# Differential and mLSTM head outputs made with tokens on the partitions, normed per token and then turned; a projection unit in spare banks, products amid halves

## The chip, the cores and the metric

The kernel runs on one core of one Trainium2 chip. The metric is the device time of one execution in microseconds (us), the median of several runs. The profile is of one further execution.

## What is computed

Two transformer blocks, one after the other, on 256 tokens of width 2048 in float32. Most of the work is the projections: x of (256, 2048) times w_in, w_br, w_out, w_up, w_down and the gates of each block. The change touches the outputs of two kinds of heads. In the first block, four differential heads:

```python
attn = (pr[:, :, 0] - lam * pr[:, :, 1])            # two softmaxes
ob = einsum('bhqk,bhkd->bhqd', attn, v)             # (256 tokens, 256 features) a head
ob = rmsnorm(ob, sub_g) * (1.0 - lambda_init)       # over the 256 features of the head
yb = ob.reshape(B, S, 1024) @ w_br_diff
```

In the second block, four mLSTM heads, which the kernel computes in one piece over all 256 tokens (here as weights W that hold all gates and decays):

```python
s = (q @ k.T) * W
h = (s @ v) / max(abs(s.sum(-1)), exp(-m))          # one divisor for each token
ha = rms_norm(h, mlstm_out_g) * sigmoid(mo)         # over the 256 features of the head
x = x + concat([ha, hb], -1) @ w_out
```

## The kernel before

**Blocks and stages.** Every weight block passes through the same pipe. SP's queue loads 128x2048 words into `raw`. A *half* is half of such a load, 128x1024. ScalarE copies the half to `split` as a rounded high part (`hi`, L562), VectorE subtracts to get the low part (`lo`, L1157), and TensorE multiplies high and low parts with X (`blocks`, L1989 and L1991, or `wide_tile`, L1999 to L2001, for the form with wide rows). `split` has a ring of four halves, so that `hi` of a half waits until TensorE has used the half four before it, and it is called three halves ahead (`LEAD = 3`): at step m of a stage ScalarE and VectorE make half m + 3.

**Order of the work.** Everything is written out by hand, engine by engine; there is no scheduler. `each_half` exists once for each engine. For each half m of a stage ScalarE does `hi(m)`, at the end of a unit `evac(m)` (a copy of half of the banks to `cross`, L568), and then `after(m)`; VectorE does `lo(m)` and then `after(m)`; TensorE does `before(m)`, waits for `lo_done` and then does the half's 16 matmuls. Each engine runs its own list strictly in this order, and semaphores tie the lists together.

**A head of diff or mlstm** is a pass over 16 halves: four units of projections (q, k, v, gate), four halves each. Late in the pass the small products of attention stand between the halves. `score` is before half 12 (diff), `turn_probs` before half 14, and before half 15 `weigh_tiles` multiplies V (stationary) with the turned probabilities, so that o comes out with features on partitions, in banks 2 and 3 of `pw`. VectorE copies o to MX (`o_raw`); ScalarE squares it (`o_square`, L666). The norm over features is then a sum over partitions, made by TensorE in the next pass before half 2: `sum_o` multiplies a matrix of ones with the squares (L2127, L2128). After it, at the same step 2, ScalarE takes the root of 256 columns (`o_norm`, L670, with a load of the root's table), VectorE the reciprocal (L1355), the products with gain and norm (L1443; with the gate for mlstm, L1761 and L1764), and both make high and low parts of the result in X2 (`o_pair`, `o_lo_pair`). TensorE does not need X2 before half 12.

```python
        def sum_o(n):

            pe.wait_ge(o_squares, n + 1)
            MM(pw[:, 1, 0:TOK], ones, MX[:, 2, :], start=True, stop=False)
            MM(pw[:, 1, 0:TOK], ones, MX[:, 3, :], start=False, stop=True).then_inc(o_sums, 1)
```

For mlstm the divisor is a further product with ones (`weigh(1, ...)`), an absolute value (L979), a maximum and a reciprocal over 256 columns (L1748, L1750). At step 15 of a pass ScalarE takes the sigmoid of the gate unit (L679 in `gate_a`, L983 in mlstm), which waits for VectorE's evacuation of unit 3 (L1170, L1172) and loads the sigmoid's table.

The outputs of diff(0), diff(1) and diff(2) are finished in the next pass of the loop, that of diff(3) in the first pass of branch; those of mlstm(0) to mlstm(2) in the next pass, that of mlstm(3) in the first pass of fox. That makes eight such places.

**proj1 and proj2** are four units of two tiles each, `proj_unit`. Units take the two pairs of banks of `ps` in turn, so each waits until the unit two before it has been evacuated (ScalarE, L781), and turns of h (`turn_normed`, L2057) stand between them.

Of the kernel before, what the change touches and what calls it, by code (L numbers as in the profile page):

```python
# [27 lines left out]
P = 128  # L28
# [142 lines left out]
def two_blocks(nc, a, out):  # L171
# [47 lines left out]
    qk_sums, qk_norms = small[:, 32:40], small[:, 40:48]  # L219

    x_squares = [E[:, 4 * c:4 * c + 4, :] for c in range(4)]

    G_MAX, G_FLOOR, G_DECAY = G[:, 0:4, :], G[:, 4:8, :], G[:, 8:16, :]
# [26 lines left out]
    def vec(name, k):  # L250
# [27 lines left out]
    o_raw, o_squares, o_sums, o_root, o_normed, o_hi, o_ready = (sem(n) for n in ("o_raw", "o_squares", "o_sums", "o_root", "o_normed", "o_hi", "o_ready"))  # L278
    sig_done, gated, ple_gated, out_ready = (sem(n) for n in ("sig_done", "gated", "ple_gated", "out_ready"))
    conv_done, hid_done, hid_hi, hid_ready = (sem(n) for n in ("conv_done", "hid_done", "hid_hi", "hid_ready"))  # L280
    max_rows_left, floor_rows_left, decay_rows_left = (sem(n) for n in ("max_rows_left", "floor_rows_left", "decay_rows_left"))
    max_rows_landed, floor_rows_landed, decay_rows_landed = (
        sem(n) for n in ("max_rows_landed", "floor_rows_landed", "decay_rows_landed"))
    gates, gate_split_hi, gate_split_lo = sem("gates"), sem("gate_split_hi"), sem("gate_split_lo")
    wt_arg, wt_done, pt_gated, den_done, den_abs = (sem(n) for n in ("wt_arg", "wt_done", "pt_gated", "den_done", "den_abs"))
# [205 lines left out]
    def _(pool):  # L491
# [39 lines left out]
        pool.wait_ge(gates, 23)  # L531
        pool.dma_start(gate_rows[4:8, :], GR[0:4, 3]).then_inc(floor_rows_left, 16)
        pool.wait_ge(max_rows_left, 16)
        pool.dma_start(G_MAX, gate_rows[0:4, :].partition_broadcast(P)).then_inc(max_rows_landed, 16)
        pool.wait_ge(floor_rows_left, 16)
        pool.dma_start(G_FLOOR, gate_rows[4:8, :].partition_broadcast(P)).then_inc(floor_rows_landed, 16)
# [10 lines left out]
    def _(act):  # L547
# [124 lines left out]
        def o_pair(k, n, tile):  # L672
            act.wait_ge(o_normed, n + 1)
            A(X2[:, bass.ds(tile, 2), 0, :], MX[:, 0:2, :], ACT.Copy).then_inc(o_hi, 1)
# [23 lines left out]
        def diff(i):  # L698
            s = At("diff", i, 8, 4)

            def after(m):
                if m == 12:
                    softmax_exps(2 * i + 8)
                if m == 13:
                    copy_pt(8 + i, 1)
                if m == 15:
                    o_square(i)
# [5 lines left out]
        def finish_diff(j):  # L713

            o_norm(j)
            o_pair(8 + j, j, 8 + 2 * j)
# [3 lines left out]
        def branch(i):  # L720
            s = At("branch", i, 8, 6)

            def after(m):
                if isinstance(i, int) and i == 0 and m == 2:
                    finish_diff(3)
# [47 lines left out]
        def proj_unit(at, u, g0):  # L773
# [7 lines left out]
            A(E_tok[:, :, columns(u)], ps[:, 2 * s:2 * s + 2, :], ACT.Copy).then_inc(evac_done, 1)  # L781
# [4 lines left out]
        proj_unit(s, 1, 0)  # L786
        hi(s, 1)
        gained_hi(2, 0, "g_mlp_pre")
# [132 lines left out]
        proj_unit(s, 2, 2)  # L921
        hi(s, 2)
        proj_unit(s, 3, 2)
        gained_hi(4, 1, "mix_norm_g_2")
# [7 lines left out]
        def gate_steps(m):  # L932
# [24 lines left out]
            if m == 10:  # L957
                gate_step(23, GR[0:4, 3], GR[0:4, 2], ACT.Exp, scale=-1.0)
                gate_step(25, small[:, 48:56], pw[:, 0, 0:8], ACT.Copy)

        def mlstm(i):
# [4 lines left out]
            def after(m):  # L966
                if first:
                    gate_steps(m)
                elif m == 2:
                    finish_mlstm(i - 1)  # L970
# [6 lines left out]
                if m == (14 if first else 13):  # L977
                    act.wait_ge(den_done, i + 1)
                    A(rn[:, 0, :], pw[:, 1, 0:TOK], ACT.Abs).then_inc(den_abs, 1)  # L979
                    o_square(i + 4)  # L980
# [5 lines left out]
        def finish_mlstm(j):  # L986
            o_norm(j + 4)
            o_pair(12 + j, j + 4, 2 * j)
# [3 lines left out]
        def fox(i):  # L992
# [20 lines left out]
            def after(m):  # L1013
# [15 lines left out]
                if i == 0 and m == 2:  # L1029
                    finish_mlstm(3)  # L1030
# [114 lines left out]
    def _(dve):  # L1145
# [212 lines left out]
        def o_lo_pair(k, tile):  # L1358
            dve.wait_ge(o_hi, k + 1)
            TT(X2[:, bass.ds(tile, 2), 1, :], MX[:, 0:2, :], X2[:, bass.ds(tile, 2), 0, :], ALU.subtract).then_inc(o_ready, 1)  # L1360
# [40 lines left out]
        def diff(i):  # L1401
# [14 lines left out]
            def after(m):  # L1416
# [14 lines left out]
                if m == 15:  # L1431
                    dve.wait_ge(pv_done, 8 + i + 1)
                    nc.vector.tensor_copy(MX[:, 0:2, :], pw[:, 2:4, 0:TOK]).then_inc(o_raw, 1)
                    evac_normed(s, 3, t[:, (s.u + 3) % 2], mix_rn)
                if m == 2 and not isinstance(i, int):
                    finish_diff(i - 1)
            each_half(s, MIX, after)

        def finish_diff(n):

            o_inverse_root(n)
            for j in range(2):
                ins = STT(MX[:, j, :], MX[:, j, :], g_sub_scaled[:, j:j + 1], rn[:, 1, :], ALU.mult, ALU.mult)  # L1443
            ins.then_inc(o_normed, 1)
            o_lo_pair(8 + n, 8 + 2 * n)
# [3 lines left out]
        def branch(i):  # L1449
            s = At("branch", i, 8, 6)  # L1450

            def after(m):
                if isinstance(i, int) and i == 0 and m == 2:
                    finish_diff(3)
# [207 lines left out]
        add_normed(5, 1, of_G(1))  # L1662
        gained_lo(4, 0, "mix_norm_g_2")
        lo(s, 1)
        add_normed(5, 2, of_G(2))
        gained_lo(4, 1, "mix_norm_g_2")
        lo(s, 2)
# [48 lines left out]
        def mlstm(i):  # L1716
# [3 lines left out]
            def after(m):  # L1720
                if m == 2 and not first:
                    finish_mlstm(i - 1)
# [20 lines left out]
                if m == (14 if first else 13):  # L1743

                    if first:
                        dve.wait_ge(floor_rows_landed, 16)
                    dve.wait_ge(den_abs, i + 1)
                    steps.step(TT(rn[:, 1, :].unsqueeze(1), rn[:, 0, :].unsqueeze(1), G_FLOOR[:, bass.ds(i, 1), :], ALU.max))  # L1748
                    settled()
                    steps.step(nc.vector.reciprocal(rn[:, 1, :], rn[:, 1, :]))  # L1750
                    settled()
                    dve.wait_ge(pv_done, 13 + i)
                    TT(MX[:, 0:2, :], pw[:, 2:4, 0:TOK], over(rn[:, 1, :], 2), ALU.mult).then_inc(o_raw, 1)
# [4 lines left out]
        def finish_mlstm(n):  # L1758
            o_inverse_root(n + 4)
            for j in range(2):  # L1760
                steps.step(STT(MX[:, j, :], MX[:, j, :], cols[:, bass.ds(col["mlstm_out_g_2"] + j + 2 * n, 1)], rn[:, 1, :], ALU.mult, ALU.mult))  # L1761
            settled()
            dve.wait_ge(sig_done, 16 + n + 1)
            TT(MX[:, 0:2, :], MX[:, 0:2, :], sg, ALU.mult).then_inc(o_normed, 1)  # L1764
            o_lo_pair(12 + n, 2 * n)
        mlstm(0)
        loop(dve, steps, 4, 10, mlstm, start=1)

        def fox(i):
# [30 lines left out]
            def after(m):  # L1800
# [25 lines left out]
                if i == 0 and m == 2:  # L1826
                    finish_mlstm(3)
# [140 lines left out]
    def _(pe):  # L1968
# [8 lines left out]
        def blocks(at, m, u, form, op, b0, tiles, first, last, tokens=(0, 1)):  # L1977

            slot = (2 * at.g + m) % RING
            s = (at.u + u) % 2  # L1980
# [479 lines left out]
```

## Time and profile before

| | |
|---|---|
| median of 3 runs | 2768.31 us (2767.82 to 2768.90) |
| the profiled execution | 2768.7 us |
| its span | 2766.9 us |
| TensorE busy | 2755.9 us, x14588 |
| VectorE busy | 1774.3 us, x2178 |
| ScalarE busy | 1384.1 us, x1819 |
| GpSimd busy | 20.5 us |

The span is the time from the first to the last record of the profiled execution; 1.8 us of its own time lie around it. Busy time counts overlapping instructions of an engine once. A mean duration of a matmul is from its start to its end and overlaps with the next; how long one holds up the queue is the distance between starts.

### The profile page before, as it was taken

Reading aid. Unit: us, or ns where it says so; the run is one execution under the profiler, and the core shown is the slowest. Engines: PE = TensorE matmul, PEld = TensorE weight load, DVE = VectorE, ACT = ScalarE, POOL = GpSimd, SP = SyncE. Lnnn points to the kernel's source line nnn. Section 1 sums busy time; section 2 is a strip of 40 time slices with the busy share of each in tenths; the row PEclk is TensorE's granted clock in tenths of the full one; section 3 lists DMA queues with packets and bytes.
Section 4 is the critical chain, followed back from the end, with each engine's and each line's share of the span. In section 5 each row is a group of like instructions: output and inputs, shape, how many; then the busy total and the mean of one; then the engine's idle time right before and its main releaser. Section 6 shows DMA issues by size and latency. Waiting matters only on the chain.

```text
span 2766.9 us, 39689 instructions
## 1 busy us (share of the span) xinstructions
PE 2755.9 (100%) x14588; PEld 2356.5 (85%) x14588; DVE 1774.3 (64%) x2178; ACT 1384.1 (50%) x1819; POOL 20.5 (1%) x36
## 2 busy tenths in 40 slices
PE   9999999999999999999999999999999999999999
PEld 7888888888888888888887888888888888888887
DVE  7666766666655656556576667665776477657655
ACT  6455554446544434444466555654544344444454
POOL 0000000000000000000000000000000000000000
PEclk9999999999999999999999999999999999999999
DMA  8555555565655565555656655555565556555654
GB/s 290 182 173 182 168 170 184 189 201 181 198 192 182 198 197 182 197 186 195 211 174 204 198 167 177 164 172 183 176 194 197 193 177 194 195 182 187 231 183 143
DMA packets 413371, 521.97 MB, mean 189 GB/s; under 512 B 8561, under 2 KB 320321, under 8 KB 412641
## 3 DMA queue, kind: packets, MB, share of 16 engines
q1 hardware_dynamic: 410528, 510.64, 56.2%
q0 software_dynamic: 2752, 10.11, 1.3%
q8 instruction: 59, 0.97, 0.1%
q14 instruction: 32, 0.25, 0.0%
HBM read 516.51 MB, written 4.21 MB: 188 GB/s over the span
## 4 chain that ended last, share of the span: by engine, by line
PE 97%; DVE 1%; ACT 1%; issue 0%; DMA 0%; SPq 0%; ACTq 0%; DVEq 0%
PE ps L1989 40%; PE ps L1991 20%; PE ps L1999 11%; PE ps L2001 11%; PE ps L2000 11%; PE pw L2110 1%; PE pw L2057 0%; PE pw L2111 0%; PE pw L2105 0%; PE pw L2099 0%; DMA raw<-in_w_in 0%; PE pw L2327 0%; DVE split L1157 0%; PE pw L2286 0%; PE pw L2098 0%
## 5 line engine op out<-in xcount | busy, mean ns | idle before, releaser
L1157 DVE TENSOR_TENSOR split<-raw,split 128x1024 fp32r<-128x1024 f32 x960 | 1154.5, 1222 | 677.5 <-ACT split L562 671.9
L562 ACT ACTIVATE split<-raw 128x1024 fp32r<-128x1024 f32 x960 | 1002.9, 1055 | 794.8 <-PE ps L2001 445.8
L1989 PE MATMUL ps<-X,split 128*128 128x512 f32 x4096 | 1292.5, 397 | 1.0 <-DVE split L1157 0.8
L1991 PEld LDWEIGHTS ps<-X,split 128*128 128x128 f32 x4096 | 769.4, 188 | 181.8
L1991 PE MATMUL ps<-X,split 128*128 128x256 f32 x4096 | 805.0, 278 | 0.0
L1989 PEld LDWEIGHTS ps<-X,split 128*128 128x128 f32 x4096 | 625.7, 189 | 4.3 <-issue 2.6
L1999 PE MATMUL ps<-split,X 128*128 128x512 f32 x1408 | 550.1, 391 | 1.9 <-ACT E L781 1.2
L2001 PE MATMUL ps<-split,X 128*128 128x512 f32 x1408 | 548.1, 389 | 0.0
L2000 PE MATMUL ps<-split,X 128*128 128x512 f32 x1408 | 547.9, 389 | 0.0
L1999 PEld LDWEIGHTS ps<-split,X 128*128 128x128 f32 x1408 | 264.3, 188 | 57.2 <-ACT E L781 1.6
L2001 PEld LDWEIGHTS ps<-split,X 128*128 128x128 f32 x1408 | 264.3, 188 | 55.1
L2000 PEld LDWEIGHTS ps<-split,X 128*128 128x128 f32 x1408 | 264.4, 188 | 54.3
L1989 PE MATMUL ps<-split,X 128*128 128x512 f32 x768 | 243.5, 398 | 0.0
L568 ACT ACTIVATE cross<-ps 128x512 f32<-128x512 f32 x160 | 95.6, 598 | 249.1 <-PE ps L1991 249.1
L1991 PEld LDWEIGHTS ps<-split,X 128*128 128x128 f32 x768 | 144.3, 188 | 34.1
L1991 PE MATMUL ps<-split,X 128*128 128x256 f32 x768 | 151.0, 278 | 0.0
L1989 PEld LDWEIGHTS ps<-split,X 128*128 128x128 f32 x768 | 117.3, 189 | 0.8 <-issue 0.4
L1170 DVE TENSOR_TENSOR t<-ps,cross 128x512 f32<-128x512 f32 x74 | 51.1, 691 | 84.6 <-ACT cross L568 84.6
L821 ACT ACTIVATE X<-t 128x512 f32 (+1 forms) x32 | 20.2, 632 | 75.6 <-DVE t L1549 75.6
L1170 DVE TENSOR_TENSOR E<-ps,cross 128x512 f32<-128x512 f32 x45 | 31.0, 689 | 36.3 <-ACT cross L568 35.1
L1551 DVE TENSOR_TENSOR X<-t,X 128x512 f32 (+1 forms) x32 | 22.2, 692 | 32.2 <-ACT X L821 32.2
L1086 ACT ACTIVATE X<-t 128x512 f32 (+1 forms) x22 | 13.9, 632 | 52.4 <-DVE t L1899 52.4
(247 smaller groups left out, 1106.4 us busy)
## 6 DMA issues: line engine op xcount, KB each, us to landing
raw<-in_w_up SPq DMA_DIRECT2D x152, 1024.0 KB, 5.5
raw<-in_w_in SPq DMA_DIRECT2D x134, 1024.0 KB, 5.1
raw<-in_w_down SPq DMA_DIRECT2D x108, 1024.0 KB, 5.1
raw<-in_w_out SPq DMA_DIRECT2D x32, 1024.0 KB, 5.1
raw<-in_w_ple_gate SPq DMA_DIRECT2D x32, 1024.0 KB, 5.1
raw<-in_w_br_moba SPq DMA_DIRECT2D x8, 1024.0 KB, 5.4
raw<-in_w_br_diff SPq DMA_DIRECT2D x8, 1024.0 KB, 5.2
raw<-in_w_ple_proj SPq DMA_DIRECT2D x4, 1024.0 KB, 5.8
```

The costliest lines, as they stand in the source:

```text
L562: A(split[:, k % RING, :, 0, :], raw[:, (k // 2) % RING, HALF * (k % 2):HALF * (k % 2) + HALF, :], ACT.Copy).then_inc(hi_done, 1)
L568: A(cross[:, s], ps[:, 2 * s:2 * s + 2, TOK:512], ACT.Copy).then_inc(cross_done, 1)
L821: A(X2[:, bass.ds(4 * i + 2 * u, 2), 0, :], t[:, (s.u + u) % 2], ACT.Copy).then_inc(hid_hi, 1)
L1157: TT(split[:, k % RING, :, 1, :], raw[:, (k // 2) % RING, HALF * (k % 2):HALF * (k % 2) + HALF, :], split[:, k % RING, :, 0, :], ALU.subtr ...
L1170: steps.step(TT(dst, ps[:, 2 * s:2 * s + 2, 0:TOK], cross[:, s], ALU.add))
L1551: TT(X2[:, bass.ds(4 * i + 2 * u, 2), 1, :], tile, X2[:, bass.ds(4 * i + 2 * u, 2), 0, :], ALU.subtract).then_inc(hid_ready, 1)
L1989: MM(ps[:, 2 * s + j, :], stay[:, 0, j * P:j * P + P], move, start=start, stop=False, skip_group_check=True)
L1991: ins = MM(ps[:, 2 * s + j, 0:TOK], stay[:, 1, j * P:j * P + P], move[:, 0, :], start=False, stop=stop, skip_group_check=True)
L1999: MM(dst, x_hi, w[:, :, 0, :], start=start, stop=False, skip_group_check=True)
L2000: MM(dst, x_hi, w[:, :, 1, :], start=False, stop=False, skip_group_check=True)
L2001: ins = MM(dst, x_lo, w[:, :, 0, :], start=False, stop=stop, skip_group_check=True)
L2110: MM(pw[:, bank, 0:TOK], values(0), pt[:, 0:TOK], start=True, stop=False, skip_group_check=True)
```

## The change

- **Outputs with tokens on the partitions.** `weigh_tokens` takes the place of `weigh_tiles`: the turned probabilities are stationary and V moves, so o comes out as (token, feature), two blocks of 128 tokens, in banks 2 and 3 of `pw`. For mlstm the divisor is a 257th column, a product with one column of ones (`den=True`). It is not copied out: it stays in `pw`.
- **Norm per token.** ScalarE squares each block straight from `pw` with a running sum (`accum_out`), at the place of the old `o_square`. The root of the two sums (`o_norm`) is now at step 0 of the next pass, after `hi(0)`. VectorE's reciprocal and the scaling of both blocks into MX (`o_scale`) are at step 1, after `lo(1)`. The divisor's absolute value, maximum and reciprocal are over two columns.
- **Then turned.** Before half 2 TensorE turns the scaled blocks (`turn_o`, four transposes) in the place of `sum_o`. At step 2 ScalarE and VectorE make the high and low parts in X2, with gain and, for mlstm, gate.
- **The floor of the divisor** is turned on TensorE with the other gate columns; its way through DRAM (two DMAs of GpSimd's queue) goes.
- **A projection unit in spare banks.** Unit 1 of proj1 and unit 2 of proj2 go to banks 2 and 3 of `pw`, without waiting for `ps`; the next turn into these banks waits for the evacuation. Some `hi`, `lo` and gain steps around them change places.
- **Products amid halves.** In diff, `turn_probs` and `weigh_tokens` stand in the middle of halves 14 and 15 (after two of four tiles) and no longer before them.

```diff
@@ ScalarE
-        def o_square(n):
-            act.wait_ge(o_raw, n + 1)
-            A(MX[:, 2:4, :], MX[:, 0:2, :], ACT.Square).then_inc(o_squares, 1)
+        def o_square(n, scale=(1.0, 1.0)):
+            for q in range(2):
+                ins = A(junk[:, q * TOK:q * TOK + TOK], pw[:, 2 + q, 0:TOK], ACT.Square, scale=scale[q], accum_out=o_sq[:, q:q + 1])
+            ins.then_inc(o_squares, 1)
 
         def o_norm(n):
-            act.wait_ge(o_sums, n + 1)
-            A(rn[:, 0, :], pw[:, 1, 0:TOK], ACT.Sqrt, bias=eps_col, scale=1.0 / 256).then_inc(o_root, 1)
+            act.wait_ge(o_squares, n + 1)
+            A(o_rms, o_sq, ACT.Sqrt, bias=eps_col, scale=1.0 / 256).then_inc(o_root, 1)
...
-                if m == 2 and not isinstance(i, int):
-                    finish_diff(i - 1)
+                if m in (0, 2) and not isinstance(i, int):
+                    finish_diff(i - 1, m)
...
+        def finish_diff(j, m):
+
+            if m == 0:
+                o_norm(j)
+            if m == 2:
+                act.wait_ge(o_turned, j + 1)
+                for f in range(2):
+                    ins = A(X2[:, bass.ds(8 + 2 * j + f, 1), 0, :], pw[:, 1, f * TOK:f * TOK + TOK].unsqueeze(1), ACT.Copy, scale=g_sub_scaled[:, f:f + 1])
+                ins.then_inc(o_hi, 1)
@@ VectorE
-        def o_inverse_root(n):
+        def o_scale(n, more=None):
             dve.wait_ge(o_root, n + 1)
-            steps.step(nc.vector.reciprocal(rn[:, 1, :], rn[:, 0, :]))
+            steps.step(nc.vector.reciprocal(o_inv, o_rms))
             settled()
...
+            for q in range(2):
+                by = o_inv[:, q:q + 1]
+                if more is None:
+                    ins = nc.vector.tensor_scalar(MX[:, q, :], pw[:, 2 + q, 0:TOK], by, None, ALU.mult)
+                else:
+                    ins = nc.vector.tensor_scalar(MX[:, q, :], pw[:, 2 + q, 0:TOK], by, more[:, q:q + 1], ALU.mult, ALU.mult)
+            ins.then_inc(o_scaled, 1)
...
+        def finish_diff(n, m):
+
+            if m == 1:
+                o_scale(n)
+            if m == 2:
+                dve.wait_ge(o_hi, 8 + n + 1)
+                for f in range(2):
+                    ins = STT(X2[:, bass.ds(8 + 2 * n + f, 1), 1, :], pw[:, 1, f * TOK:f * TOK + TOK].unsqueeze(1), g_sub_scaled[:, f:f + 1],
+                              X2[:, bass.ds(8 + 2 * n + f, 1), 0, :], ALU.mult, ALU.subtract)
+                ins.then_inc(o_ready, 1)
@@ TensorE
+                if amid and m >= 14:
+                    blocks(at, m, u, form, op, 0, range(k0, k0 + 2), first, False)
+                    amid(m)
+                    blocks(at, m, u, form, op, 2, range(k0 + 2, k0 + per), False, last).then_inc(half_used, 1)
...
-        def weigh_tiles():
-            for j in range(2):
-                ins = weigh(2 + j, lambda key, j=j: V[:, key, j * P:j * P + P], PT[:, 0])
+        def weigh_tokens(den=False):
+
+            for q, blocks_of_q in enumerate((((0, 0),), ((P, 0), (TOK, 1)))):
+                for n, (c, key) in enumerate(blocks_of_q):
+                    stay = PT[:, 0, c:c + P]
+                    ins = MM(pw[:, 2 + q, 0:TOK], stay, V[:, key, :], start=n == 0, stop=n == q, skip_group_check=True)
+                    if den:
+                        ins = MM(pw[:, 2 + q, TOK:TOK + 1], stay, ones[:, 0:1], start=False, stop=n == q, skip_group_check=True)
             ins.then_inc(pv_done, 1)
 
-        def sum_o(n):
-
-            pe.wait_ge(o_squares, n + 1)
-            MM(pw[:, 1, 0:TOK], ones, MX[:, 2, :], start=True, stop=False)
-            MM(pw[:, 1, 0:TOK], ones, MX[:, 3, :], start=False, stop=True).then_inc(o_sums, 1)
+        def turn_o(n):
+
+            pe.wait_ge(o_scaled, n + 1)
+            for f in range(2):
+                for q in range(2):
+                    ins = T(pw[:, 1, f * TOK + q * P:f * TOK + q * P + P], MX[:, q, f * P:f * P + P], ident)
+            ins.then_inc(o_turned, 1)
...
         proj_unit(s, 0, X2, 12)
         proj_unit(s, 1, X2, 12)
-        proj_unit(s, 2, X2, 12)
+        proj_unit(s, 2, X2, 12, pw[:, 2:4, :])
         turn_normed(4, 2, 0)
         proj_unit(s, 3, X2, 12)
+        pe.wait_ge(evac_done, U0["proj2"] + 3)
         turn_normed(4, 2, 1)
```

How the change moves instructions is shown at the place on which most of the prediction rests, the start of a pass of the diff loop, on three engines. Line numbers of the changed kernel differ a little: its `hi` is L559, its `lo` L1161, its matmuls L2001 and L2003.

ScalarE before, from the end of a pass (`cross` and the squares) over the loop's branch to step 2 of the next pass; `split` is the high part that `hi` makes, L679 the sigmoid, L670 the root:

```order
L568 ACTIVATE cross<-ps 128x512 [waits half_used]
L666 ACTIVATE E<-E 128x512 [waits o_raw]
L679 ACT_TABLE_LOAD
L679 ACTIVATE G<-t 128x512 [waits evac_done]
L140 UNCONDITIONAL_BRANCH
...
L562 ACTIVATE split<-raw 128x4x256 [waits half_used]
...
L562 ACTIVATE split<-raw 128x4x256 [waits half_used]
...
L562 ACTIVATE split<-raw 128x4x256 [waits half_used]
L670 ACT_TABLE_LOAD
L670 ACTIVATE rn<-pw,small 128x256 [waits o_sums]
```

And ScalarE of the changed kernel at the same place:

```order
L565 ACTIVATE cross<-ps 128x512 [waits half_used]
L663 ACTIVATE junk,small<-pw 128x256 [waits pv_done]
L663 ACTIVATE junk,small<-pw 128x256
L673 ACT_TABLE_LOAD
L673 ACTIVATE G<-t 128x512 [waits evac_done]
...
L559 ACTIVATE split<-raw 128x4x256 [waits half_used]
L668 ACT_TABLE_LOAD
L668 ACTIVATE small<-small 128x2 [waits o_squares]
...
L559 ACTIVATE split<-raw 128x4x256 [waits half_used]
...
L559 ACTIVATE split<-raw 128x4x256 [waits half_used]
```

The root and its table load have moved from behind the third `hi` of the pass to behind the first; the count of table loads is the same (34 in both programs).

VectorE of the changed kernel, from the last evacuation of a pass to step 2 of the next (`split` here is the low part, made by `lo`; before, three of them stood ahead of the reciprocal):

```order
L1176 TENSOR_TENSOR t<-t,acc 128x512 [waits dve_steps]
L140 UNCONDITIONAL_BRANCH
...
L1161 TENSOR_TENSOR split<-raw,split 128x4x256 [waits hi_done]
...
L1161 TENSOR_TENSOR split<-raw,split 128x4x256 [waits hi_done]
L1359 RECIPROCAL small<-small 128x2 [waits o_root]
...
L1364 TENSOR_SCALAR E<-pw,small 128x256 [waits dve_steps]
L1364 TENSOR_SCALAR E<-pw,small 128x256
...
L1161 TENSOR_TENSOR split<-raw,split 128x4x256 [waits hi_done]
```

The scaling stands behind the second `lo`, which takes the high part of the second `hi`.

TensorE at the boundary of half 1 and half 2 before, where E are the squares in MX and con the ones:

```order
L1991 MATMUL ps<-X,split 128x256 x2
L2127 MATMUL pw<-E,con 128x256 [waits o_squares]
L2128 MATMUL pw<-E,con 128x256
...
L1989 MATMUL ps<-X,split 128x512 [waits lo_done]
```

And in the changed kernel, where E are the scaled blocks in MX:

```order
L2003 MATMUL ps<-X,split 128x256 x2
L2151 MATMUL pw<-con,E 128x128 [waits o_scaled]
L2151 MATMUL pw<-con,E 128x128 x3
...
L2001 MATMUL ps<-X,split 128x512 [waits lo_done]
```

The small work stands at the same place of TensorE's list, but what it waits for is no longer the squares of the last pass: it is the scaling of the step before.

## Rows read from the trace of the kernel before

**Rows 1.** Page, parts 1, 2 and 4: busy time, granted clock, and the chain's engines

```profile
PE 2755.9 (100%) x14588; PEld 2356.5 (85%) x14588; DVE 1774.3 (64%) x2178; ACT 1384.1 (50%) x1819; POOL 20.5 (1%) x36
...
PEclk9999999999999999999999999999999999999999
...
PE 97%; DVE 1%; ACT 1%; issue 0%; DMA 0%; SPq 0%; ACTq 0%; DVEq 0%
```

**Rows 2.** Groups of TensorE's matmuls by line; behind the bar busy us, mean ns, idle before

```profile
L1999 PE MATMUL ps<-split,X 128*128 128x512 f32 x1408 | 550.1, 391 | 1.9 <-ACT E L781 1.2 <-DVE X L1200 0.4 <-DVE G L1503 0.2
...
L2105 PE MATMUL pw<-con,E 128*128 128x128 f32 x60 | 8.7, 276 | 1.9 <-DVE E L1414 1.9
```

**Rows 3.** Timeline of TensorE at half 2 of diff(2): start us, us, line, tiles

```profile
305.93 0.40 PE L1991 MATMUL ps<-X,split 128*128 128x256 f32 x2
...
306.63 0.39 PE L1991 MATMUL ps<-X,split 128*128 128x256 f32 x2
306.86 0.59 PE L2127 MATMUL pw<-E,con 128*128 128x256 f32 x2
...
308.18 0.40 PE L1991 MATMUL ps<-X,split 128*128 128x256 f32 x2
```

**Rows 4.** Timeline of TensorE at half 15 of diff(1), the products with V

```profile
297.18 0.59 PE L2110 MATMUL pw<-E 128*128 128x256 f32 x2
297.61 0.38 PE L2111 MATMUL pw<-E 128*128 128x128 f32 x2
```

**Rows 5.** Timeline of TensorE, set-up: one fp32 product of two columns

```profile
34.27 0.28 PE L2090 MATMUL pw<-small,con 128*128 128x2 f32 x2
```

**Rows 6.** Timeline of ScalarE from the end of half 15 of diff(1)

```profile
301.48 0.60 ACT L568 ACTIVATE cross<-ps 128x512 f32<-128x512 f32 x1 [3.04 <-PE ps L1991]
...
303.67 1.28 ACT L679 ACT_TABLE_LOAD   x1 [1.07 <-DVE t L1172]
...
305.51 2.94 ACT L562 ACTIVATE split<-raw 128x1024 fp32r<-128x1024 f32 x3
308.46 1.28 ACT L670 ACT_TABLE_LOAD   x1
309.76 0.47 ACT L670 ACTIVATE rn<-pw,small 128x256 f32<-128x256 f32 x1
```

**Rows 7.** Timeline of VectorE in the same stretch

```profile
306.58 3.50 DVE L1157 TENSOR_TENSOR split<-raw,split 128x1024 fp32r<-128x1024 f32 x3 [3.05 <-ACT split L562]
```

**Rows 8.** Timeline of ScalarE in out1: a root of two columns

```profile
669.18 0.29 ACT L591 ACTIVATE norm_root<-norm_ms,small 128x2 f32<-128x2 f32 x1
```

**Rows 9.** Timeline of VectorE: scaling by a column, and a small reciprocal

```profile
288.03 0.35 DVE L1180 TENSOR_SCALAR E<-E,norm_col 128x256 f32<-128x256 f32 x1
...
292.28 0.18 DVE L1407 RECIPROCAL small<-small 128x4 f32<-128x4 f32 x1 [1.37 <-ACT E L650]
```

**Rows 10.** Timeline of ScalarE: an activation with a running sum, and its reading

```profile
291.66 0.49 ACT L650 ACTIVATE E<-E,small 128x256 f32<-128x256 f32 x1
292.06 0.19 ACT L650 ACTIVATION_READ_ACCUMULATOR E<-E,small 128x1 f32 x1
```

**Rows 11.** Timeline of ScalarE at the end of diff(0)

```profile
252.37 0.60 ACT L568 ACTIVATE cross<-ps 128x512 f32<-128x512 f32 x1 [2.70 <-PE ps L1991]
...
255.34 1.99 ACT L562 ACTIVATE split<-raw 128x1024 fp32r<-128x1024 f32 x2
```

**Rows 12.** Timeline of ScalarE at the end of mlstm(1)

```profile
1601.97 0.60 ACT L568 ACTIVATE cross<-ps 128x512 f32<-128x512 f32 x1 [1.73 <-PE ps L1991]
...
1604.59 1.99 ACT L562 ACTIVATE split<-raw 128x1024 fp32r<-128x1024 f32 x2
```

**Rows 13.** Timeline of ScalarE at the end of mlstm(0)

```profile
1557.27 2.94 ACT L562 ACTIVATE split<-raw 128x1024 fp32r<-128x1024 f32 x3
```

**Rows 14.** Timeline of TensorE at half 2 of mlstm(1)

```profile
1558.56 0.59 PE L2127 MATMUL pw<-E,con 128*128 128x256 f32 x2
```

**Rows 15.** Timeline of TensorE from the span's start: the products of zeros

```profile
1.50 8.68 PE L2073 MATMUL pw<-junk 128*128 128x512 f32 x16 [1.50 <-DVE junk L1263]
```

More of the change, by code:

```diff
@@ L1720, in after @@
             def after(m):
-                if m == 2 and not first:
-                    finish_mlstm(i - 1)
+                if m in (1, 2) and not first:
+                    finish_mlstm(i - 1, m)
                 if first and m <= 4:
@@ L1756, in mlstm, with finish_mlstm @@
             each_half(s, MIX, after)
[L1758 to L1765, printed above, removed]
+        def finish_mlstm(n, m):
+            if m == 1:
+                o_scale(n + 4, o_den)
+            if m == 2:
+                dve.wait_ge(o_turned, n + 5)
+                dve.wait_ge(sig_done, 16 + n + 1)
+                for f in range(2):
+                    ins = STT(MX[:, 2 + f, :], pw[:, 1, f * TOK:f * TOK + TOK], cols[:, bass.ds(col["mlstm_out_g_2"] + f + 2 * n, 1)], sg[:, f, :], ALU.mult, ALU.mult)
+                ins.then_inc(o_gated, 1)
+                dve.wait_ge(o_hi, 12 + n + 1)
+                TT(X2[:, bass.ds(2 * n, 2), 1, :], MX[:, 2:4, :], X2[:, bass.ds(2 * n, 2), 0, :], ALU.subtract).then_inc(o_ready, 1)
         mlstm(0)
-        loop(dve, steps, 4, 10, mlstm, start=1)
+        loop(dve, steps, 4, 9, mlstm, start=1)
         def fox(i):
@@ L1975, in unit_start, with blocks @@
                 pe.wait_ge(evac_done, k)
-        def blocks(at, m, u, form, op, b0, tiles, first, last, tokens=(0, 1)):
+        def blocks(at, m, u, form, op, b0, tiles, first, last, tokens=(0, 1), banks=None):
             slot = (2 * at.g + m) % RING
             s = (at.u + u) % 2
+            banks = ps[:, 2 * s:2 * s + 2, :] if banks is None else banks
             for n, kt in enumerate(tiles):
@@ L2002, in wide_tile, with each_half @@
             return ins
-        def each_half(at, rows, ready=None, before=None, start=0):
+        def each_half(at, rows, ready=None, before=None, start=0, amid=None):
             for m, (u, form, op, k0, per, first, last) in list(enumerate(rows))[start:]:
@@ L2157, in before, with amid @@
                     score(2 * i + 8)
+                if m == 2 and not isinstance(i, int):
+                    turn_o(i - 1)
+            def amid(m):
                 if m == 14:
@@ L2162, in before @@
                     pe.wait_ge(pt_ready, 8 + i + 1)
-                    weigh_tiles()
-                if m == 2 and not isinstance(i, int):
-                    sum_o(i - 1)
-            each_half(s, MIX, None, before)
+                    weigh_tokens()
+            each_half(s, MIX, None, before, amid=amid)
         diff(0)
@@ L2172, in finish_diff @@
             if m == 2:
-                sum_o(3)
+                turn_o(3)
             if m == 7:
@@ L2331, in before @@
                     pe.wait_ge(evac_done, s.unit(2) + 1)
[L2332 to L2333 removed]
+                    weigh_tokens(den=True)
             each_half(s, MIX, x1_is(4), before)
@@ L2363, in before @@
                 if i == 0 and m == 2:
-                    sum_o(7)
+                    turn_o(7)
                 if i == 1:
```

136 lines of the change are left out of this document (62 added, 74 removed).

## The prediction

> **What bounds the kernel now.** I read the page first, then TensorE's waits by line, then the timelines of all three engines around the places that the change edits. TensorE is busy for 2755.9 of 2766.9 us at full granted clock and is 97% of the chain that ended last [rows 1]. Its idle time before matmuls is a few microseconds in all: in the wide form 1.9 us, of which 1.2 wait for ScalarE's evacuation in a projection (L781) and 0.2 for VectorE, and 1.9 us before `turn_probs` (L2105), in diff [rows 2]. VectorE and ScalarE are busy 64% and 50% of the span. So only two things count: what TensorE itself executes, where a microsecond less is one gained, and any new wait of TensorE, where it is one lost. The reader should not look at the 1.75 us reciprocals or the wide roots that vanish from VectorE and ScalarE; no wait of TensorE ends on them.
>
> **TensorE's own work.** Costs are distances between starts, since matmuls overlap.
>
> - `sum_o`: from the last L1991 group ahead of it to the next of its kind behind it is 1.55 us (306.63 to 308.18) [rows 3]. A tile's period without it is 0.70 (305.93 to 306.63), so it costs 0.85. `turn_o` is four transposes. L2105 is 8.7 us for 60, 0.145 each [rows 2], so 0.55 to 0.6. Gain 0.3, eight times: -2.4 us.
> - `weigh_tiles` is two products of 256 columns at 0.43 (297.18 to 297.61) [rows 4] and two of 128, half as many columns, at 0.22: 1.30. `weigh_tokens` is three of 256: 1.29. Nothing.
> - The divisor of mlstm: before one product of 256 and one of 128, 0.65; now three of one column. The nearest row is a product of two columns, two passes in 0.28 [rows 5]: 0.14 each if they overlap as others do, 0.28 if not, so 0.42 to 0.84. Four times: between -0.9 and +0.8; I take -0.5.
> - Two more small transposes with the gates: +0.2, bounds 0 and 0.3 by the 0.145 above.
> - Products amid halves 14 and 15 of diff: two tiles, 1.4 us, now cover the wait for VectorE's combination, of which there is 1.9 us in all in four passes [rows 2]. -1.9 us. The next thing late would be ScalarE's copy of the turned probabilities, which has the rest of half 14 and two tiles of half 15.
> - The projection units: the waits of 1.2 and 0.2 us go [rows 2]: -1.4 us. Nothing if the later wait for the spare banks takes their place; ScalarE is ready about when TensorE is, so I keep the gain and note the bound.
> - The floor's two DMAs, the table loads (as many as before) and everything on VectorE that becomes shorter: nothing, since TensorE's waits [rows 2] don't end there.
>
> Sum: -2.4 - 0.5 + 0.2 - 1.9 - 1.4 = -6.0 us.
>
> **The new wait.** `turn_o` stands where `sum_o` stood, before half 2, but waits for something made much later. `sum_o` waited for squares made at the end of the last pass. `turn_o` waits for `o_scaled`, and that stands in VectorE's list behind `lo(1)`, which needs `hi(1)`, which now stands on ScalarE behind the root with its table load. ScalarE is late at just this place. In the diff loop it takes `cross` at 301.48, then waits for the evacuated gate unit, loads the sigmoid's table at 303.67, and begins `hi(0)` only at 305.51 [rows 6]. TensorE meanwhile has matrices made three halves ahead, and reaches the end of half 1 at 306.86 [rows 3], 5.38 us after `cross` began. That lateness costs nothing before, because the low part of half 3 is not needed before 306.86 + 0.85 + 4 x 0.70 = 310.5.
>
> From the start of `hi(0)`, here s, the changed lists give step by step:
>
> - `hi(0)`, 1.05 us (a third of the 2.94, plus the overlap) [rows 6];
> - the table load and the way to the root's start, 308.46 to 309.76: 1.30 [rows 6];
> - the root of two columns, 0.29 long [rows 8], of which the next instruction overlaps 0.1: 0.2;
> - `hi(1)` until VectorE's `lo(1)` starts: 305.51 to 306.58 is 1.07 [rows 6, 7];
> - `lo(1)`: 1.15, a third of 3.50 rounded down for the overlap [rows 7];
> - the reciprocal of two columns, 0.2, and two scalings of 256 columns at 0.35, the second overlapping: 0.62 [rows 9];
> - the semaphore to TensorE: 0.06.
>
> That is 5.65 us. `turn_o` can start at s + 5.65.
>
> - diff(1), diff(2) and diff(3): s = 305.51, so 311.16 against 306.86: TensorE stands for **4.3 us**, three times 12.9.
> - diff(0): s = 255.34 with `cross` at 252.37 [rows 11]. Here the sigmoid's load does not wait for the gate unit, so ScalarE's own work ahead of it counts: two squares with their sums, about 0.68 each [rows 10], against one square of about 0.6 before. s becomes 256.0 and the start 261.7; TensorE is there 5.38 after `cross`, at 257.75: 3.95 us. Bounds 3.3 and 4.0.
> - mlstm(1) to mlstm(3): `cross` 1601.97, s = 1604.59 [rows 12]; 1610.24 against 1607.35: **2.9 us**, three times 8.7. The squares stand two halves earlier here, so they don't delay s.
> - mlstm(0): s = 1557.27 [rows 13], TensorE there at 1558.56 [rows 14]; that gives 4.4. The chain ahead of `cross` is shorter now (a wide reciprocal goes from it), which I put at 0.6: 3.8 us. Bounds 3.6 and 4.4.
>
> Sum +29.35 us. Behind `turn_o` on TensorE stand half 2 and all the rest of the program, so all of it is lost: the ring of four halves lets nothing be made ahead during the stall that TensorE could take instead, and it has no idle time later in which to give it back. ScalarE's and VectorE's steps at m = 2 come a little later than before, but are short, and `hi(3)` waits for half 2 anyway.
>
> Together +29.35 - 6.0 = +23.3 us. On the profiled execution's 2768.7 that is 2792.0; its time stands 0.4 above the median shown, so a median of 2791.7, as a round number 2792.
>
> **The price of the table load.** The trace shows the root starting 1.30 us after its table load starts, and the `split` before it ending where the load begins [rows 6]. By the Trainium skill ("ScalarE: Activation LUTs", What ACT_TABLE_LOAD costs) a switch of sets costs about 2.66 us, since a drain of about 1.38 us comes with the load. The loads of these rows show no such drain. By that page every one of the eight chains would be 1.38 us longer and the sum 11 us higher, some 2803; I go by the rows.
>
> **Rivals.**
>
> - *The clock falls after the stalls.* Before, TensorE never stands for more than the 1.5 us at the start, and its granted clock is full throughout [rows 1], so the trace holds no stall like the new ones. After the idle start 16 products of 512 columns take 8.68 us [rows 15]; at the pace of a 256-column pass, 0.215, they would take 16 times 0.43, 6.9 us. So 1.8 us is what one slow beginning costs. Should the long stalls, four to eight of them, each be followed by one, 7 to 14 us come on top: 2799 to 2806. Against it: the stalls are short beside the passes, and TensorE is otherwise always busy. 15 in 100. The Trainium skill ("TensorE: Matmul & The Clock Gate", Why this matters for your kernels) warns that a pause between bursts of matmuls can take the clock back to half; the trace of before can't show whether 4.3 us are enough.
> - *TensorE does not wait, and the change is faster.* If ScalarE came to `hi(0)` 4.3 us earlier in the diff loop and 2.9 in mlstm, `o_scaled` would be in time. Only below that point does the stall vanish at all; each microsecond less is 8 us less in sum. Then the -6.0 remain: 2762. What would do it is a sigmoid that no longer holds up `hi(0)`; nothing in the lists moves it. 4 in 100.
> - *Only part of the wait.* The order of the three lists is fixed, so a stall can be shorter only by durations. If my chain is 1 us too long everywhere, 2784; if the mlstm places are hidden for a reason that I don't see, 2783. If the gains on TensorE don't show either, 2798. These lie in my forecast's own range, 2783 to 2798, for which I give 76 in 100, the forecast in its middle. 3 in 100 for a sum near no change (2763 to 2774, some of the stalls missing), 2 in 100 for the longer chains above, around 2803.
>
> **Range and chances.** The range is 2783 to 2804: from a chain 1 us shorter up to most of the clock's case. A measurement of this kernel can tell about 0.2%, 5.5 us, from no change. Faster by more 0.04, within 0.02, slower 0.94.
>
> **What the profile after would show.** Right: a wait of TensorE at L2151 (`turn_o`) on VectorE's L1364, eight times, 29 us in all, in two sizes near 4.3 and 2.9; on ScalarE the L668 table load directly behind `hi(0)`; no wait at the transposes of `turn_probs`; TensorE's idle share up from 11 to near 37 us; busy time about 3 us lower. A granted clock under full behind the stalls, or tiles of more than 0.70 us for some microseconds, speaks for the first rival. The prediction is wrong if L2151 has no wait, or if another wait goes that I hold for hidden.

## The result

| | before | changed |
|---|---|---|
| median | 2768.58 us | 2806.53 us (2804.30 to 2808.57, 4 runs) |
| ratio | | 1.0137, 95% interval 1.0125 to 1.0149 |
| the profiled execution | 2768.7 us | 2808.57 us |
| its span | 2766.9 us | 2806.7 us |
| mean granted clock | 1.00 | 0.991 |

The changed kernel is 38 us slower; forecast were 23 more, 2792, with a range up to 2804. So the direction was as said, the amount was 15 us short, and the time lies 2.5 us above the range. The profiled execution lies 2 us above the median, and its mean granted clock is the lowest of the four, 0.991 against 0.994 in the one of 2804.30 us.

The busy line of the changed kernel's page, which answers to [rows 1]:

```profile
PE 2770.1 (99%) x14582; PEld 2368.7 (84%) x14582; DVE 1754.0 (62%) x2186; ACT 1388.9 (49%) x1844; POOL 19.5 (1%) x34
```

TensorE's idle time is 36.6 us, as said (near 37). Against the prediction, its busy time did not fall by 3 us but rose by 14, with six instructions fewer. The page's line of the clock does not show why: it has a 9 in all 40 slices, as before, since a digit stands for 70 us and 9 for 90% and more. The mean clock of the core, 0.991, does.

TensorE's waits in the changed kernel (us in total, times, longest); L2151 is `turn_o`, L1364 and L1366 are the scaling for diff and for mlstm:

```profile
PE pw L2151 <- DVE E L1364: 16.7, 4, 4.4
PE pw L2151 <- DVE E L1366: 12.9, 4, 3.5
```

Eight waits, 29.5 us; 29.35 had been worked out. The rest of the list is 2.3 us, 1.5 of them at the program's start. The waits of [rows 2] that the change was to take away, for L1414 in diff and L781 in proj2, are gone. The chain of the wait, on ScalarE, at the end of diff(1), which answers to [rows 6]:

```profile
310.29 1.05 ACT L559 ACTIVATE split<-raw 128x1024 fp32r<-128x1024 f32 x1
311.36 1.28 ACT L668 ACT_TABLE_LOAD   x1
312.65 0.30 ACT L668 ACTIVATE small<-small 128x2 f32<-128x2 f32 x1
312.85 1.99 ACT L559 ACTIVATE split<-raw 128x1024 fp32r<-128x1024 f32 x2
```

and on VectorE behind it, which answers to [rows 7]:

```profile
313.93 1.23 DVE L1161 TENSOR_TENSOR split<-raw,split 128x1024 fp32r<-128x1024 f32 x1 [1.33 <-ACT split L559]
315.07 0.16 DVE L1359 RECIPROCAL small<-small 128x2 f32<-128x2 f32 x1
315.26 0.88 DVE L1364 TENSOR_SCALAR E<-pw,small 128x256 f32<-128x256 f32 x2
```

Read from top to bottom: `hi(0)`, the root's table load, the root, `hi(1)`, then `lo(1)`, reciprocal, scaling. From 310.29 to TensorE's turn at 316.19 that is 5.90 us, against 5.65 worked out. The scaling is the difference: 0.88 for the two out of `pw`, not 0.62, which was priced by a row with its input in another tile [rows 9].

TensorE at the same place, which answers to [rows 3]:

```profile
311.41 0.40 PE L2003 MATMUL ps<-X,split 128*128 128x256 f32 x2
316.19 1.11 PE L2151 MATMUL pw<-con,E 128*128 128x128 f32 x4 [4.38 <-DVE E L1364]
316.96 1.20 PE L2001 MATMUL ps<-X,split 128*128 128x512 f32 x2
317.96 0.63 PE L2003 MATMUL ps<-X,split 128*128 128x256 f32 x2
...
319.24 0.63 PE L2003 MATMUL ps<-X,split 128*128 128x256 f32 x2
...
320.52 0.63 PE L2003 MATMUL ps<-X,split 128*128 128x256 f32 x2
...
321.53 0.40 PE L2003 MATMUL ps<-X,split 128*128 128x256 f32 x2
...
322.24 0.40 PE L2003 MATMUL ps<-X,split 128*128 128x256 f32 x2
```

Behind the wait the tiles come every 1.28 us (317.96 to 319.24 to 320.52) and then every 0.70 again (321.53 to 322.24). The granted clock of this stretch (columns: busy us and count of each engine, PEclk, share of DMA, GB/s):

```profile
311.81:313.81 2.00, 0.00 (x0) 0.00 (x0) 0.79 (x1) 1.99 (x4) 0.00 (x0) 1.00 0.00 0
313.81:316.19 2.38, 0.00 (x0) 0.00 (x0) 2.23 (x5) 1.03 (x2) 0.00 (x0) 0.62 0.92 275
316.19:318.19 2.00, 2.00 (x8) 1.80 (x9) 1.08 (x1) 0.71 (x2) 0.00 (x0) 0.50 0.57 198
318.19:320.19 2.00, 2.00 (x8) 1.71 (x8) 0.88 (x2) 0.12 (x1) 0.00 (x0) 0.50 0.78 219
320.19:322.19 2.00, 2.00 (x10) 1.78 (x9) 0.00 (x0) 0.23 (x1) 0.00 (x0) 0.75 0.88 306
```

The clock fell to 0.50, the 1.2 GHz level, while TensorE stood, and came back 5.0 us after it had begun again. Behind all eight waits there is such a slow stretch, and it ends 2.8 to 6.0 us after TensorE has begun again. In seven places the clock fell inside the wait. In the eighth, in fox, it was full during the whole wait and fell 1.1 us after TensorE had begun again:

```profile
1740.36:1743.47 3.11, 0.00 (x0) 0.00 (x1) 2.35 (x5) 1.64 (x2) 0.00 (x0) 1.00 0.77 232
1743.47:1753.47 10.00, 10.00 (x50) 8.73 (x51) 5.21 (x9) 3.25 (x4) 0.00 (x0) 0.83 0.44 139
```

From the last L2003 ahead of each wait to the fourteenth behind it, less the wait itself and fourteen tiles at 0.6975, 22.5 us are left over in sum, 1.9 to 3.4 at a place. In the kernel before the same sum, with `sum_o`, is 6.8.

### The profile page after: what moved, and what is told of

It reads as the page before. It is cut to its first block, busy times and chain, and to the rows that moved or that the text cites. A ratio compares the mean times of both kernels' runs of the same rounds, so it can differ in the third digit from the quotient of the medians.

```text
span 2806.7 us, 39707 instructions
## 1 busy us (share of the span) xinstructions
PE 2770.1 (99%) x14582; PEld 2368.7 (84%) x14582; DVE 1754.0 (62%) x2186; ACT 1388.9 (49%) x1844; POOL 19.5 (1%) x34
## 4 chain that ended last, share of the span: by engine, by line
PE 97%; ACT 1%; DVE 1%; issue 1%; ACTq 0%; DVEq 0%
PE ps L2001 39%; PE ps L2003 20%; PE ps L2011 11%; PE ps L2012 11%; PE ps L2013 11%; PE pw L2074 1%; ACT split L559 1%; PE pw L2141 0%; PE pw L2116 0%; PE pw L2090 0%; ACT L668 0%; PE pw L2151 0%; PE pw L2127 0%; PE pw L2122 0%; PE pw L2115 0%
## 5 line engine op out<-in xcount | busy, mean ns | idle before, releaser
L1161 DVE TENSOR_TENSOR split<-raw,split 128x1024 fp32r<-128x1024 f32 x960 | 1156.5, 1223 | 728.4 <-ACT split L559 723.4
L559 ACT ACTIVATE split<-raw 128x1024 fp32r<-128x1024 f32 x960 | 1005.6, 1057 | 827.4 <-PE ps L2013 444.9
L2001 PE MATMUL ps<-X,split 128*128 128x512 f32 x4096 | 1302.3, 399 | 0.4 <-DVE split L1161 0.2
L2003 PEld LDWEIGHTS ps<-X,split 128*128 128x128 f32 x4096 | 775.5, 189 | 184.0
L2003 PE MATMUL ps<-X,split 128*128 128x256 f32 x4096 | 809.5, 279 | 0.0
L2001 PEld LDWEIGHTS ps<-X,split 128*128 128x128 f32 x4096 | 631.4, 190 | 2.6 <-issue 1.3
L2001 PE MATMUL ps<-split,X 128*128 128x512 f32 x768 | 244.5, 400 | 0.0
L2003 PEld LDWEIGHTS ps<-split,X 128*128 128x128 f32 x768 | 145.0, 189 | 34.3
L2003 PE MATMUL ps<-split,X 128*128 128x256 f32 x768 | 151.6, 279 | 0.0
L2001 PEld LDWEIGHTS ps<-split,X 128*128 128x128 f32 x768 | 117.9, 190 | 0.8 <-issue 0.4
```

Of the source, the lines that this page charges most:

```text
L559: A(split[:, k % RING, :, 0, :], raw[:, (k // 2) % RING, HALF * (k % 2):HALF * (k % 2) + HALF, :], ACT.Copy).then_inc(hi_done, 1)
L1161: TT(split[:, k % RING, :, 1, :], raw[:, (k // 2) % RING, HALF * (k % 2):HALF * (k % 2) + HALF, :], split[:, k % RING, :, 0, :], ALU.subtr ...
L2001: MM(ps[:, 2 * s + j, :], stay[:, 0, j * P:j * P + P], move, start=start, stop=False, skip_group_check=True)
L2003: ins = MM(ps[:, 2 * s + j, 0:TOK], stay[:, 1, j * P:j * P + P], move[:, 0, :], start=False, stop=stop, skip_group_check=True)
```

## The experiments

In their expectations "18.7 us" is the 22.5 just named less 3.8, eight turns at 0.47. Below it is split into 17.4 us of the clock and some 1.4 us, in sum, that the waits cost beside their idle time, called their restart. Each run is compared with the kernel before as it was timed beside it, 2768.93 us in the first four and 2768.75 in the last three.

**The turn two halves later.** All three lists move together, TensorE's `turn_o` and what VectorE and ScalarE (there `m in (0, 2)` becomes `m in (0, 4)`) do behind it; diff's edit stands for all. In fox the turn moves by one half only, to half 3, since VectorE needs the tiles at step 3.

```diff
-                if m == 2 and not isinstance(i, int):
+                if m == 4 and not isinstance(i, int):
                     turn_o(i - 1)
...
-                if m in (1, 2) and not isinstance(i, int):
+                if m in (1, 4) and not isinstance(i, int):
                     finish_diff(i - 1, m)
```

> Only the place of the turn moves: before half 4 of the next pass (half 3 in fox, where VectorE needs the tiles at step 3) instead of before half 2, with the high and low parts that follow it. Theory: TensorE's 29.5 us at turn_o are a wait for o_scaled, and the slow tiles behind each wait are the clock that the wait cost. Two halves more are 5.6 us, more than the longest wait of 4.4, so both go: no wait at turn_o but 0.1 to 0.4 in fox, granted clock 1.00 throughout, 2806.5 - 29.5 - 18.7 = 2758, at most 2762. Rival, that the wait only moves (to o_ready before half 12, or to a late low part because ScalarE and VectorE do these steps beside others): 2775 or more. Rival, that the new form of the outputs is itself slower on TensorE: above 2768.

Measured: 2760.21 us, ratio to before 0.997 (0.9958 to 0.9981). Mean clock 1.00. The page's busy line:

```profile
PE 2751.0 (100%) x14582; PEld 2353.8 (85%) x14582; DVE 1751.7 (64%) x2186; ACT 1385.6 (50%) x1844; POOL 19.6 (1%) x34
```

and, of TensorE's waits, the only one at the turn, in fox:

```profile
PE pw L2151 <- DVE E L1366: 0.3, 1, 0.3
```

The turn in the diff loop, now between full tiles:

```profile
310.41 0.40 PE L2003 MATMUL ps<-X,split 128*128 128x256 f32 x2
310.64 0.60 PE L2151 MATMUL pw<-con,E 128*128 128x128 f32 x4
...
311.56 0.40 PE L2003 MATMUL ps<-X,split 128*128 128x256 f32 x2
```

1.15 us from L2003 to L2003, less a tile's 0.70: the turn costs 0.45, where `sum_o` cost 0.85 [rows 3]. So the same instructions, with nothing but the turn's place changed, give 46 us back and are 8.7 us faster than the kernel before. Both rivals fall: the wait does not come up elsewhere, and the new form of the outputs is not slower.

**Filling the wait.** Six products of 384 columns that nothing reads (four in mlstm) ahead of the wait, with the turn where the change has it.

```diff
-        def turn_o(n):
+        def turn_o(n, fill=6):
 
+            for _ in range(fill):
+                MM(pw[:, 0, 0:384], ones, mask, start=True, stop=True)
             pe.wait_ge(o_scaled, n + 1)
```

> The changed kernel with products that nothing reads put before the wait at turn_o: six fp32 products of 384 columns in diff, four in mlstm, some 3.9 and 2.6 us at full clock, into a bank that is free there. TensorE is then occupied in most of the stall and waits 0.5 us at its end. If the slow tiles come from TensorE's standing still, the clock stays at 1.00 and the time is 2806.5 - 18.7 = 2788 (2786 to 2791). If they come from the turn itself (transposes, reading what VectorE has just written) or from the other engines' work at this place, the slow tiles stay and the time is about 2806.

Measured: 2790.81 us, ratio to before 1.0079 (1.0064 to 1.0095). Mean clock 1.00. TensorE at diff's end:

```profile
309.30 4.04 PE L2149 MATMUL pw<-con 128*128 128x384 f32 x12
313.85 0.66 PE L2153 MATMUL pw<-con,E 128*128 128x128 f32 x4 [0.51 <-DVE E L1364]
...
314.80 0.40 PE L2003 MATMUL ps<-X,split 128*128 128x256 f32 x2
...
315.50 0.39 PE L2003 MATMUL ps<-X,split 128*128 128x256 f32 x2
```

The turn begins as late as in the changed kernel, but the tiles behind it take 0.70 from the first on, all eight times, and the kernel is 15.7 us faster than the changed one (17.2 by the spans of the profiled executions) with 40 products (80 records) more. So the slow tiles are the clock's, and the clock falls because TensorE stands; neither the turn nor the other engines' work brings them.

**Scaling at step 0.** VectorE scales behind `lo(0)`, which takes `hi(1)` and `lo(1)` out of the chain.

```diff
-            if m == 1:
+            if m == 0:
                 o_scale(n)
```

> VectorE's reciprocal and scaling stand behind lo(0) instead of behind lo(1); the turn stays before half 2. hi(1) and lo(1) leave the chain, 2.2 us at each place: the waits become 1.35, three of 2.2, 1.3 and three of 0.9, 11.9 in sum. Theory, by its wait alone: 17.6 us come back. The clock is the open part: if waits this short do not lower it, 18.7 more come back and the time is 2770; if each still does, 2789. My first theory of the chain, that the root's table load and hi(0) are in it, is wrong if the waits vanish altogether.

Measured: 2776.76 us, ratio to before 1.0029 (1.0018 to 1.004). The waits:

```profile
PE pw L2151 <- DVE E L1364: 8.4, 4, 2.3
PE pw L2151 <- DVE E L1366: 4.5, 4, 1.4
```

12.9 us against 11.9 expected: the chain is the right one, and the root with its load is in it. The clock gave neither of the two answers. Five waits of 1.0 to 1.5 us and one of three of 2.3 us left it alone; behind the other two of 2.3 us it fell, and only once TensorE was at work again, by 1.2 us in the place shown and by 0.4 us in the other:

```profile
309.33 0.66 PE L2151 MATMUL pw<-con,E 128*128 128x128 f32 x4 [2.30 <-DVE E L1364]
...
310.29 0.40 PE L2003 MATMUL ps<-X,split 128*128 128x256 f32 x2
...
311.34 0.63 PE L2003 MATMUL ps<-X,split 128*128 128x256 f32 x2
...
312.62 0.63 PE L2003 MATMUL ps<-X,split 128*128 128x256 f32 x2
```

**The turn one half later**, before half 3 everywhere: the edit of the first experiment with 3 for 4.

> The turn before half 3 in all eight places: each wait shorter by one half, 2.8 us: 0.75, three of 1.6, 0.7, three of 0.3, 7.2 in sum. If waits up to 1.6 us leave the clock alone: 2806.5 - 22.4 - 18.7 = 2765.5. If the long three still lower it, about 2773. Together with the run that scales at step 0 this gives a second length of wait.

Measured: 2768.38 us, ratio 0.9998 (0.9989 to 1.0008). The waits are 5.5 and 1.7 us in sum (diff, mlstm), the longest 1.6, as expected, and the clock is 1.00; but the time is 3 us above 2765.5. The tiles say why:

```profile
308.65 0.40 PE L2003 MATMUL ps<-X,split 128*128 128x256 f32 x2
310.65 0.66 PE L2151 MATMUL pw<-con,E 128*128 128x128 f32 x4 [1.60 <-DVE E L1364]
...
311.60 0.40 PE L2003 MATMUL ps<-X,split 128*128 128x256 f32 x2
```

From L2003 to L2003 are 2.95 us, less the wait of 1.60 and a tile 0.65. A turn with a wait ahead of it leaves 0.64 us over on the mean, one without leaves 0.44: 0.2 us of restart at each wait, which my figure of 18.7 had counted with the clock. Most of it is a matter of counting. Without a wait the turn starts 0.17 us before the last product ends (310.64 against 310.41 + 0.40, in the first experiment), and a wait is counted from that end. From the measured 2760.2: 6.9 us of waits more and seven restarts, 1.4, is 2768.5.

**Products amid halves alone**, put into the kernel before; `weigh_tiles` moves in the same way into half 15, and the products themselves stay as they were:

```diff
-                if m == 14:
-                    turn_probs(8 + i, 1)
...
+            def amid(m):
+                if m == 14:
+                    turn_probs(8 + i, 1)
```

> The kernel before with one part of the change alone: in diff, the turned probabilities and the products with V stand in the middle of halves 14 and 15. The wait of 0.48 us in each of four passes should be covered by the two tiles ahead: -1.9 us by the wait alone, up to -2.8 with the restart of TensorE's queue behind it (the pass of the diff loop is 1.13 us shorter with the whole change and the turn before half 4, of which the turn is 0.42 and the wait 0.48). So 2766 to 2767. Rival, that the gain is in the form of the products (three of 256 columns for four) and not in the place: 2768.5.

Measured: 2765.87 us, ratio 0.999 (0.9981 to 0.9999), that is -2.9 us. The wait on L1414 [rows 2] is gone, 1.9 us in four passes, and with it one of 0.2 us for a low part in the first of them. The rest, 0.8 us, is about what five restarts of 0.2 would make. The products were not changed in form, so the gain is that of the place.

**The old projections** in the version with the turn before half 4. The unit of proj1 and the order of the steps around both stages go back in the same way:

```diff
-        proj_unit(s, 2, X2, 12, pw[:, 2:4, :])
+        proj_unit(s, 2, X2, 12)
         turn_normed(4, 2, 0)
         proj_unit(s, 3, X2, 12)
-        pe.wait_ge(evac_done, U0["proj2"] + 3)
```

> The version with the turn before half 4, with the projection units as in the kernel before (all four in the usual banks, the old order around them). TensorE's waits of 1.2 us in proj2 and 0.2 in proj1 come back: 2760.2 + 1.4 = 2761.6, up to 2762.1 if the 0.3 us wait for a low part right behind comes back as well. Rival, that the wait for the spare banks had taken their place and the unit brings nothing: 2760.2.

Measured: 2762.91 us, ratio 0.9979 (0.997 to 0.9988): 2.7 us slower than with the spare banks. These waits are back:

```profile
PE ps L2011 <- ACT E L781: 1.2, 1, 1.2
PE ps L2001 <- DVE split L1161: 0.6, 2, 0.3
...
PE ps L2011 <- DVE G L1511: 0.2, 1, 0.2
```

1.2, 0.2 and 0.4 of the split's are 1.8; three or four restarts of about 0.2 make it some 2.5, an estimate. So the units in the spare banks, with the order around them, are worth more than the 1.4 put down for them.

**The root ahead of the sigmoid.** The turn stays before half 2; ScalarE takes the root right behind the squares and VectorE scales at step 15.

```diff
                     o_square(i)
+                    o_norm(i)
                     gate_a(s, i + 4)
...
                     evac_normed(s, 3, t[:, (s.u + 3) % 2], mix_rn)
+                    o_scale(i)
```

> The other way to be in time: the turn stays before half 2, but ScalarE takes the root right behind the squares, at step 15 of the old pass (13 or 14 in mlstm), ahead of the sigmoid, and VectorE scales at step 15 behind the last evacuation. Then hi(0), hi(1), lo(0) and lo(1) are no longer in the chain: in diff the root is done about 3.4 us after the copy to cross starts, the scaling about 4.3, and TensorE comes at 5.4. If the place of root and scaling in the two lists is the whole cause, no wait at turn_o and a full clock: 2760, no slower than the turn before half 4. The price is hi(0) 1.5 us later behind a second table load: its low part is then done 7.7 us after cross starts, and TensorE wants it at 8.6. Rival: it is late, and TensorE waits before half 3, each time by up to 1 us: 2764 to 2768.

Measured: 2759.84 us, ratio 0.9967 (0.9955 to 0.9979). No wait at the turn in any of the eight places, mean clock 1.00. ScalarE and TensorE at the end of diff(1):

```profile
301.38 1.28 ACT L668 ACT_TABLE_LOAD   x1
302.67 0.30 ACT L668 ACTIVATE small<-small 128x2 f32<-128x2 f32 x1
302.99 1.28 ACT L673 ACT_TABLE_LOAD   x1
304.28 0.63 ACT L673 ACTIVATE G<-t 128x512 f32 x1
304.82 2.94 ACT L559 ACTIVATE split<-raw 128x1024 fp32r<-128x1024 f32 x3
```

```profile
305.18 0.40 PE L1999 MATMUL ps<-X,split 128*128 128x256 f32 x2
305.41 0.60 PE L2147 MATMUL pw<-con,E 128*128 128x128 f32 x4
...
306.32 0.40 PE L1999 MATMUL ps<-X,split 128*128 128x256 f32 x2
```

The root is done 2.4 us before the turn. `hi(0)` starts 4.8 us after `cross` (at 300.03), 0.8 later than before the change [rows 6] and not 1.5, since the sigmoid had waited 1.07 us for its unit before. This is a second remedy of the same cause, from the other side, and no slower than the first (0.4 us apart, with ranges of single runs that overlap).

## Why the prediction was wrong

- **What bounds, and what to ignore.** Right. 20 us of work left VectorE and no one waited less for it; TensorE's own work and waits explain all of the time.
- **TensorE's own work, -6.0 us.** Right in sign, too small: without the stall it is -8.7 (turn before half 4). By the experiments products amid halves are -2.9, not -1.9; the projection units -2.7, not -1.4; what is left by subtraction, -3.1, is put down to the new form of the outputs, where -2.4 for the turn and about nothing for the rest were put down. The turn itself is eight times 0.41, -3.3. The divisor by columns of ones brought nothing that shows (a pass of the mlstm loop is 0.42 us shorter, which is the turn alone). The common part of the error: a removed wait also saves about 0.2 us of restart, and I priced the removed waits by their idle time only.
- **The new wait, +29.35 us.** Right in its mechanism and its eight places, and near in its sum: 4.4 for 4.3 in the diff loop, 3.5 for 3.95 behind diff(0), 3.5 for 3.8 behind mlstm(0), 3.1 for 2.9 in the mlstm loop. That the sum came out at 29.5 is in part luck, for the two numbers are not the same thing: 29.35 was worked out from start to start, 29.5 is idle time from the end of the last product. From start to start TensorE came to the turn 4.55, 3.71, 3.69 and 3.28 us late, 30.9 us in all. Of the 1.5 us too little most is the scaling out of `pw` (0.88 us for two in diff and 0.99 in mlstm, for 0.62); behind diff(0) and mlstm(0) ScalarE's list, priced too long, took part of it back.
- **The price of the table load.** The measurement decides for the rows: 311.36 to 312.65 is 1.29 us from load to root, with no drain, against the 2.66 us that the Trainium skill ("ScalarE: Activation LUTs", What ACT_TABLE_LOAD costs) gives. The rival that hung on it, 2803, is 3.5 us below the measured time, and its mechanism did not occur.
- **The rival of the clock: this is the step that failed.** The forecast's sum has no term for the clock. The case stood among the rivals, priced at 7 to 14 us and given 15 in 100, "against it: the stalls are short beside the passes, and TensorE is otherwise always busy". All eight stalls lowered the clock, also those of 3.1 us. Its size: 22.5 us left over at the eight places, less eight turns with restart at 0.64, is **17.4 us**, 1.3 to 2.8 for each stall, 2.2 in the mean, where the slow start [rows 15] had given 1.8. These are figures of the profiled execution; at the median, 2 us lower, the clock's share is by estimate some 15 us, 17.4 less these 2, and filling the wait gave 15.7 back. That a stall is short beside its pass did not keep the clock up in any of the eight places. The Trainium skill's warning ("TensorE: Matmul & The Clock Gate", Why this matters for your kernels), that a pause between bursts can halve the clock, was cited and then given a low chance: the trace agrees with it, 0.50 behind a wait of 4.38 us.
- **The sum again.** From the version without stalls, span 2758.3: 29.2 us of waits more, 17.4 of clock, 1.4 of restarts make 2806.3; the span is 2806.7. Against the forecast for this execution, 2792.0, the measured 2808.57 is 16.6 more: 17.4 of clock and 1.5 of the wait, less the 2.7 that TensorE's own work gave beyond the 6.0 put down, make 16.2. The range ended at 2804 because its upper end took "most of the clock's case" at too low a price. That the rival's own upper figure, 2806, is so near the median is in part luck: the gains that it left out made up for its low price. The other rivals (no wait, part of the wait, some stalls missing) did not occur.

Not settled: why two of three waits of 2.3 us lowered the clock and the third did not, and why the slow stretch was shorter behind two of the eight stalls (1.3 and 1.6 us of cost, the other six 2.1 to 2.8). No run changed the length of a single wait in small steps.

## What to carry to other kernels

When a step is moved into the list of another engine, walk the whole list ahead of it there, table loads and the work queued behind a late wait included: here a result of a few columns stood behind two high parts, a table load and a low part, and TensorE came for it before it was made. On a kernel that TensorE bounds, a stall can cost more than its idle time: here 0.2 us of restart each and, behind every stall of 3.1 us or more, 1.3 to 2.8 us more for work at half the clock. Such a consumer is cured without changing any work, by asking for the result later (two halves here) or by making it before the engine's next long wait; and an edit that is good by 8.7 us can be hidden behind a loss of 46 that comes from its place alone.

## What the runs showed of the hardware

- A stall of 3.1 to 4.4 us lowered TensorE's granted clock from 2.4 to 1.2 GHz in eight of eight places, one of 2.3 us in two of three, and stalls up to 1.6 us in none of thirteen. The fall can come inside the stall (4.38 us, clock 0.62 in its second half) or after work has begun again (behind stalls of 2.30 and 3.11 us, the clock full in the whole stall and lower 0.4 to 1.2 us after its end).
- Products that nothing reads keep the clock up: with 4.04 us of them in the stall, tiles took 0.70 us at once.
- A tile of the features form takes 0.70 us at full clock and 1.28 at half, 1.8 times.
- Scaling 256 columns out of PSUM by a column on VectorE took 0.48 us (0.88 for two in a row, which overlap), against 0.35 for the same from SBUF [rows 9].
